# Filling the attention of an even mixer with projection work, on one core of a Trainium2

## The reference, cut to what matters

```python
def even_mixer(h, w_in, gla_w_gate, gla_b_gate, gla_norm_g, fox_b_f, w_out):
    q_g, k_g, v_g, g_out, gk_low, q_f, k_f, v_f, f_logit = jnp.split(h @ w_in, EVEN_SPLITS, axis=-1)
    ...
    o_gla = gla_chunked(q_g, k_g, v_g, gk)                 # 4 heads, values of 128
    o_gla = rmsnorm(o_gla, gla_norm_g) * jax.nn.silu(g_out)  # norm over the 128 values of a head
    log_f = jax.nn.log_sigmoid(f_logit + fox_b_f)
    o_fox = fox_attention(q_f, k_f, v_f, log_f)            # 8 heads of 64, softmax, causal
    o = jnp.concatenate([o_gla, o_fox], axis=-1)
    return o @ w_out

def mixer(u, cos, sin, w_in, w_attn_br, dw_w, dw_b, cln_g, cln_b, w_conv_pw, w_out):
    # second block: attention of 8 heads, a depthwise convolution of 31 taps, two gates
    ...
```

## Time and profile before

| what | value |
|---|---|
| median of three runs | 1800.25 us (1794.48 to 1805.85) |
| time of the profiled execution | 1797.06 us |
| its span | 1795.3 us, 27915 instructions |
| TensorE busy | 1742.4 us (97%) |
| VectorE busy | 1373.1 us (76%) |
| ScalarE busy | 936.6 us (52%) |
| GpSimd busy | 292.9 us (16%) |
| mean DMA rate | 194 GB/s |
| mean granted TensorE clock | 0.986 of full speed |

### The profile page before, as it was taken

The page is one execution under the profiler, slowest core; times in us unless marked ns, Lnnn a source line. Parts: engine busy times, 40 slices in busy tenths (PEclk is TensorE's granted clock), DMA queues, the critical chain, the costliest instruction groups (busy, mean ns, idle before and its releaser), DMA issues.

```text
span 1795.3 us, 27915 instructions
## 1 busy us (share of the span) xinstructions
PE 1742.4 (97%) x11232; PEld 1564.8 (87%) x11232; DVE 1373.1 (76%) x1830; ACT 936.6 (52%) x1172; POOL 292.9 (16%) x219
## 2 busy tenths in 40 slices
PE   6999999999999999999999999999999999999998
PEld 5888798888888888878888898898888998998887
DVE  5997655698888978686987779878755699778654
ACT  6554454655456544466554354656543536555433
POOL 1000000130120001050000139600000089010000
PEclk9999998999999999999999999999999999999999
DMA  7777433277667766523666643343555344335551
GB/s 272 277 253 272 166 143 139 82 289 263 229 257 281 260 241 249 211 94 146 253 258 250 241 165 141 121 165 138 188 194 193 129 148 159 140 121 200 189 193 47
DMA packets 53232, 348.28 MB, mean 194 GB/s; under 512 B 6769, under 2 KB 10114, under 8 KB 13058
## 3 DMA queue, kind: packets, MB, share of 16 engines
q1 hardware_dynamic: 53122, 346.73, 52.9%
HBM read 345.65 MB, written 1.05 MB: 193 GB/s over the span
## 4 chain that ended last, share of the span: by engine, by line
PE 78%; issue 11%; POOL 5%; DVE 3%; ACT 2%; POOLq 0%; DMA 0%; SPq 0%; ACTq 0%; DVEq 0%
PE bank L927 38%; PE bank L926 20%; PE bank L882 5%; PE bank L883 4%; PE bank L884 4%; POOL arena L831 4%; DVE wl L1928 1%; ACT wh L1468 1%; PE bank L897 1%; PE bank L1401 0%; PE bank L1226 0%; PE bank L907 0%; POOL arena L833 0%; DMA raw<-in_chunks 0%; PE bank L1194 0%
## 5 line engine op out<-in xcount | busy, mean ns | idle before, releaser
L1928 DVE TENSOR_TENSOR wl<-raw,wh 128x2048 fp32r<-128x2048 f32 (+1 forms) x279 | 640.0, 2295 | 246.1 <-ACT wh L1468 245.4
L927 PE MATMUL bank<-xx,wh 128*128 128x512 f32 x1920 | 670.5, 393 | 0.0
L1468 ACT ACTIVATE wh<-raw 128x2048 fp32r<-128x2048 f32 (+1 forms) x279 | 526.2, 1886 | 209.8 <-PE bank L927 174.1
L926 PE MATMUL bank<-xx,wl 128*128 128x256 f32 x1920 | 540.7, 282 | 14.8 <-DVE wl L1928 14.8
L927 PEld LDWEIGHTS bank<-xx,wh 128*128 128x128 f32 x1920 | 360.6, 188 | 80.0
L927 PE MATMUL bank<-hx,wh 128*128 128x512 f32 x1216 | 422.0, 390 | 0.0
L926 PEld LDWEIGHTS bank<-xx,wl 128*128 128x128 f32 x1920 | 364.0, 190 | 16.1 <-issue 14.7
L926 PE MATMUL bank<-hx,wl 128*128 128x256 f32 x1216 | 343.4, 282 | 1.2 <-DVE wl L1928 1.2
L882 PE MATMUL bank<-xx,wh 128*128 128x256 f32 x1008 | 293.6, 291 | 2.5 <-ACT arena L1602 1.4
L883 PE MATMUL bank<-xx,wh 128*128 128x256 f32 x1008 | 286.8, 285 | 0.0
L884 PE MATMUL bank<-xx,wl 128*128 128x256 f32 x1008 | 286.7, 284 | 0.0
(11 more groups left out here) (329 smaller groups left out, 1962.6 us busy)
## 6 DMA issues: line engine op xcount, KB each, us to landing
raw<-in_chunks SPq DMA_DIRECT2D x263, 1024.0 KB, 4.8
arena<-in_ada SPq DMA_DIRECT2D x48, 1024.0 KB, 5.0
raw<-in_chunks SPq DMA_DIRECT2D x16, 768.0 KB, 4.2
arena<-in_bias_rows SPq DMA_DIRECT2D x1, 2048.0 KB, 17.6
x<-in_x SPq DMA_DIRECT2D x4, 256.0 KB, 4.1
arena<-in_w_uk SPq DMA_DIRECT2D x1, 1024.0 KB, 4.8
arena<-in_w_uv SPq DMA_DIRECT2D x1, 1024.0 KB, 9.0
out<-x SPq DMA_DIRECT2D x8, 128.0 KB, 2.1
```

The costliest lines, as they stand in the source:

```text
L926: pe.matmul(o[:, 0:T], lo_w, halves[:, 0, :], start=start, stop=False, skip_group_check=True)
L927: return pe.matmul(o.rearrange("p (h t) -> p h t", h=2), hi_w, halves, start=False, stop=stop, skip_group_check=True)
L1468: act.activation(wh[:, c % RING, at], raw[:, c % RING, at], ACT.Copy).then_inc(hi_made.sem, 1)
L1928: dve.tensor_tensor(wl[:, c % RING, at], raw[:, c % RING, at], wh[:, c % RING, at].bitcast(F32), ALU.subtract).then_inc(lo_made.sem, 1)
```

## The change

- **Column norm.** TensorE forms the sums of squares with the squares as weights and one column of ones (eight matmuls of one column), so that they stand as 128 x 8 values. Root and reciprocal are taken of 8 columns. A new step `spread`, after chunk 10, spreads them with eight matmuls (a column broadcast as weights, the identity moving) into banks 4 and 5; ScalarE copies both out, VectorE multiplies as before.
- **Value chunk 11** leaves the list and runs in two halves, after the scores of pair 0 and of pair 1. ScalarE copies it out and runs its `hi` at the end of round 1, VectorE its `lo` in round 2.
- **Output chunks 12 and 13**, tiles k = 0 to 3, run in rounds 2 and 3 and no longer in `pe_out`.
- **Scores** use banks 4 and 5 alone, so that scores of pair p wait for the masks of pair p - 1. `halves` moves behind the loop's first masks on VectorE and ahead of the pairs on ScalarE.
- **Mixers of the second block.** VectorE's `lo` of chunk 19, which stood ahead of the last five taps, runs behind them, next to `lo` of chunk 20.

```diff
-    SCORES = (4, 5, 2, 3)
-    EVEN = ["small", 0, "z", 1, "gk", 2, "G", 3, "decay", 4, 5, "kt", 6, "A", 7, "kv", 8, "o", 9, "norm", 10, 11, "halves"]
+    EVEN = ["small", 0, "z", 1, "gk", 2, "G", 3, "decay", 4, 5, "kt", 6, "A", 7, "kv", 8, "o", 9, "norm", 10, "spread"]
@@ pe_out
-                    if s != "odd" or (ks[0], j) != (0, 0):
+                    if ks[0] > 0 or not (s == "even" or (s == "odd" and j == 0)):
@@ pe_pairs
+            def last_values(m):
+                c = c0 + F_V + 1
+                pe.wait_ge(lo_made.sem, c + 1)
+                pe.wait_ge(proj_out.sem, proj_out.at(s, F_V))
+                ... (24 matmuls of half m into bank 3)
+                if m == 1:
+                    last.then_inc(chunk_used.sem, 1)
             def scores(p):
-                if p >= 2:
-                    pe.wait_ge(ns_made.sem, ns_made.at(s, 2 * p - 2))
+                if p == 0:
+                    pe.wait_ge(proj_out.sem, proj_out.at(s, F_K + 2))
+                    pe.wait_ge(gla_act.sem, G_ACT["orstd"])
+                    pe.wait_ge(fox_split.sem, 2)
+                else:
+                    pe.wait_ge(ns_made.sem, ns_made.at(s, 2 * p))
             def transposes(h):
+                if h == 0:
+                    pe.wait_ge(gla_dve.sem, G_DVE["o"])
             for i in range(pairs + 2):
                 if i < pairs:
                     scores(i)
+                if i < 2:
+                    last_values(i)
+                elif i < 4:
+                    pe.wait_ge(proj_out.sem, proj_out.at(s, F_V + i - 1))
+                    out_part(s, c0 + 12, range(0, 4), i - 2)
@@ pe_even
             def norm():
-                for q in range(2):
-                    last = pe.matmul(bank[4 + q][:, :], ones[:, :], osq[:, q * 512:(q + 1) * 512], start=True, stop=True)
+                for i in range(8):
+                    last = pe.matmul(bank[4][:, i:i + 1], osq[:, i * P:(i + 1) * P], ones[:, 0:1], start=(i == 0), stop=True, ...)
+            def spread_norm():
+                pe.wait_ge(gla_dve.sem, G_DVE["oinv"])
+                for i in range(8):
+                    last = pe.matmul(bank[4 + i // 4][:, (i % 4) * P:(i % 4 + 1) * P], ocol[:, 1, i:i + 1].broadcast_to((P, P)), ident[:, :],
+                                     start=True, stop=True)
-            pe.wait_ge(gla_dve.sem, G_DVE["o"])
-            pe.wait_ge(fox_split.sem, 2)
             pe_pairs(s)
@@ act_pairs
+                if s == "even" and i == 1:
+                    act_chunk(s, F_V + 1, base[s] + F_V + 1)
@@ act_even
-                act.activation(oroot[:, 0:512], bank[4][:, :], ACT.Sqrt, ...)
-                act.activation(oroot[:, 512:1024], bank[5][:, :], ACT.Sqrt, ...)
+                act.activation(ocol[:, 0, :], bank[4][:, 0:8], ACT.Sqrt, ...)
+            def spread_norm():
+                act.wait_ge(gla_pe.sem, G_PE["ospread"])
+                act.activation(orstd[:, 0:512], bank[4][:, :], ACT.Copy)
+                act.activation(orstd[:, 512:1024], bank[5][:, :], ACT.Copy).then_inc(gla_act.sem, 1)
+            halves()
             act_pairs(s)
@@ dve_pairs
+                if s == "even" and i == 0:
+                    halves()
+                if s == "even" and i == 2:
+                    lo(base[s] + F_V + 1 + RING)
@@ dve_even
-                link(dve.reciprocal(orstd, oroot))
+                dve.reciprocal(ocol[:, 1, :], ocol[:, 0, :]).then_inc(gla_dve.sem, 1)
+            def spread_norm():
+                dve.wait_ge(gla_act.sem, G_ACT["orstd"])
                 ... (lines 2216 and 2220 as before)
@@ dve_mix, last round of the attention
-                lo(c0 + 12 + 2 * p + RING)
-                convolve(TAPS_PER_STEP)
                 if p < 2:
+                    lo(c0 + 12 + 2 * p + RING)
+                    convolve(TAPS_PER_STEP)
                     lo(c0 + 13 + 2 * p + RING)
             convolve(len(taps))
             ...
+            lo(c0 + 16 + RING)
             lo(c0 + 17 + RING)
```

More of the change, by code:

```diff
@@ L284, in build @@
     AT = pj[:, 0:2, :]
-    osq, oroot, orstd = Carver(at_z).take(4 * T), Carver(at_e).take(4 * T), Carver(at_k).take(4 * T)
+    osq, ocol, orstd = Carver(at_z).take(4 * T), Carver(at_e).take(16, "p (r i) -> p r i", r=2), Carver(at_k).take(4 * T)
     c = Carver(ARENA - ATT)
@@ L511, in vec @@
         return vecT[:, tile, row:row + 1]
-    G_PE = {n: i + 1 for i, n in enumerate(["z", "G", "kt", "A", "kv", "o", "ostat"])}
-    G_ACT = {n: i + 1 for i, n in enumerate(["glow", "z", "lnz", "lnf", "gs", "decays", "keT", "osq", "oroot"])}
-    G_DVE = {n: i + 1 for i, n in enumerate(["fz", "zabs", "fabs", "gk", "fsum", "decayed", "A", "state", "o"])}
-    EVEN = ["small", 0, "z", 1, "gk", 2, "G", 3, "decay", 4, 5, "kt", 6, "A", 7, "kv", 8, "o", 9, "norm", 10, 11, "halves"]
+    G_PE = {n: i + 1 for i, n in enumerate(["z", "G", "kt", "A", "kv", "o", "ostat", "ospread"])}
+    G_ACT = {n: i + 1 for i, n in enumerate(["glow", "z", "lnz", "lnf", "gs", "decays", "keT", "osq", "oroot", "orstd"])}
+    G_DVE = {n: i + 1 for i, n in enumerate(["fz", "zabs", "fabs", "gk", "fsum", "decayed", "A", "state", "oinv", "o"])}
+    EVEN = ["small", 0, "z", 1, "gk", 2, "G", 3, "decay", 4, 5, "kt", 6, "A", 7, "kv", 8, "o", 9, "norm", 10, "spread"]
     E_K, E_Q, E_V, E_G, F_Q, F_K, F_V = 0, 1, 2, 4, 6, 8, 10
@@ L1057, in pe_pairs @@
             q, k, v, _ = att_of(s)
-            pe.wait_ge(proj_out.sem, proj_out.at(s))
-            def scores(p):
-                if p >= 2:
-                    pe.wait_ge(ns_made.sem, ns_made.at(s, 2 * p - 2))
+            c0 = base[s]
+            def last_values(m):
+                c = c0 + F_V + 1
+                pe.wait_ge(lo_made.sem, c + 1)
+                pe.wait_ge(proj_out.sem, proj_out.at(s, F_V))
+                tok = slice(m * P, (m + 1) * P)
+                for kk in range(KT):
+                    col = slice(kk * T, (kk + 1) * T)
+                    last = three(bank[3][:, m * T:(m + 1) * T], xh[:, kk, tok], xl[:, kk, tok], wh[:, c % RING, col], wl[:, c % RING, col],
+                                 start=(kk == 0), stop=(kk == KT - 1))
+                if m == 1:
+                    last.then_inc(chunk_used.sem, 1)
+            def scores(p):
+                if p == 0:
[4 more added lines that the diff above has]
+                    pe.wait_ge(ns_made.sem, ns_made.at(s, 2 * p))
                 for at, qt, kt in ((slice(0, P), slice(0, P), slice(0, P)), (slice(P, 384), slice(P, T), slice(0, T))):
                     for h in (2 * p, 2 * p + 1):
-                        pe.matmul(bank[SCORES[h % 4]][:, at], q(h)[:, qt], k(h)[:, kt], start=(at.start == 0), stop=False, skip_group_check=True)
+                        pe.matmul(bank[4 + h % 2][:, at], q(h)[:, qt], k(h)[:, kt], start=(at.start == 0), stop=False, skip_group_check=True)
                 for h in (2 * p, 2 * p + 1):
-                    b = bank[SCORES[h % 4]]
+                    b = bank[4 + h % 2]
                     pe.matmul(b[:, 0:384], selr[32:40, h, :], fhigh[32:40, :], start=False, stop=False, skip_group_check=True)
@@ L1080, in output @@
             def output(p):
+                pe.wait_ge(proj_out.sem, proj_out.at(s, F_V + 1 + p // 2))
                 pe.wait_ge(pt_out.sem, pt_out.at(s, 2 * p + 2))
@@ L1167, in norm @@
                 pe.wait_ge(gla_act.sem, G_ACT["osq"])
-                for q in range(2):
-                    last = pe.matmul(bank[4 + q][:, :], ones[:, :], osq[:, q * 512:(q + 1) * 512], start=True, stop=True)
+                for i in range(8):
+                    last = pe.matmul(bank[4][:, i:i + 1], osq[:, i * P:(i + 1) * P], ones[:, 0:1], start=(i == 0), stop=True, skip_group_check=True)
+                last.then_inc(gla_pe.sem, 1)
+            def spread_norm():
[3 more added lines that the diff above has]
+                                     start=True, stop=True)
                 last.then_inc(gla_pe.sem, 1)
             todo = {"small": small, "z": z, "G": cumulate, "kt": turn_keys, "A": scores, "kv": chunk_states,
-                    "o": outputs, "norm": norm}
+                    "o": outputs, "norm": norm, "spread": spread_norm}
             for step in EVEN:
@@ L1706, in halves @@
                                ACT.Copy).then_inc(xh_made.sem, 1)
-            todo = {"small": small, "z": z, "gk": log_sigmoid, "G": cumulated, "decay": decays, "kt": keys, "o": squares, "norm": norm, "halves": halves}
+            todo = {"small": small, "z": z, "gk": log_sigmoid, "G": cumulated, "decay": decays, "kt": keys, "o": squares, "norm": norm, "spread": spread_norm, "halves": halves}
             for step in EVEN:
@@ L2098, in link, with dve_pairs @@
             dve.wait_ge(dve_step.sem, n_step[0])
-        def dve_pairs(s):
+        def dve_pairs(s, halves=None):
             pairs = heads_of[s] // 2
@@ L2110, in masked @@
                 for b, at in enumerate((slice(0, P), slice(P, 384))):
```

(6 more changed lines are left out.)

3 lines of the change are left out of this document (1 added, 2 removed).

## The result

| | before | after |
|---|---|---|
| median of 9 runs | 1798.74 us (1794.48 to 1805.85) | 1787.14 us (1783.61 to 1792.18) |
| profiled execution, its span | 1797.06, 1795.3 us | 1791.12, 1789.4 us |
| mean granted TensorE clock | 0.986 | 0.990 |

The ratio is 0.9932, 95% interval 0.9919 to 0.9944: 10 to 14.6 us faster, where I had forecast 5.8. The two profiled executions differ by 5.9 us only; that half the gain is missing between them is part of what had to be found.

The account below looks back on a forecast made before the run. TensorE, busy 97% of the span, was taken as the bound. Even mixer 3.8 plus second-block mixers 2.0 gave 5.8 us: 1791.3 from the profiled execution, 1794.5 from the median, forecast 1794 us, range 1787 to 1801.

Parts of the forecast that it names:

- the term for the mixers of the second block: Moving `lo` of chunk 19 behind the taps gains 2.0 us in `mix0`, 0 in `mix1`; bounds together 0 and 3.
- The even mixer's 3.8: Even mixer's attention: gain 4.8 us at full clock, less 1.0 for low clock, so 3.8, between 0 and 6.5.
- The loop's end: Even mixer's attention loop ends at 328.1 at full clock; the old position of the same point was 333.1.
- 1.0 for the clock still to come: One low-clock stretch of 3.4 us behind the new wait in the even mixer, at about 7 in 10: -1.0 us.
- first wait: TensorE stands still about 1.9 us before the first scores, until ScalarE has copied the spread out behind `hi`.
- the last outputs' wait: Even mixer: the last outputs wait about 1.0 us for ScalarE to copy out two transposes.
- Column norm, 16 passes: Even mixer, TensorE: new norm's one-column matmuls take 2.0 us against 1.3 before, so +0.7 us; upper bound 2.2.
- The reading of the long stall: Even mixer's 3.25 us idle before the first transposes: VectorE's 6.55 us reciprocal puts `lo` and split late, ahead of the masks.
- Queues, two score banks, softmax beside the rounds: Later loads cost nothing; scores of pair 1 wait 0.3 us for masks; softmax fits beside 6.2 us rounds, 3 us cover.
- Rival A: Nothing to see: same TensorE work, waits return elsewhere; gain -2 to 2.5 us, 1798 to 1802; chance 0.22.
- B: Slower: low clock holds through the even mixer's attention loop; 19 us net, 1819, or 1811 with two thirds; chance 0.06.
- Rival C: More: one-column matmuls nearly free, clock doesn't fall, wait shrinks; gain 8 to 10 us, 1791; chance 0.12.

Follow-up runs that it names:

- e3: Only the move of VectorE's `lo` of chunk 19 behind the last taps in both second-block mixers, on the kernel before: 1793.74 us, ratio 0.9976.
- e2: The change without its last block, so the even mixer changed and the second block's mixers left as before: 1791.47 us, ratio 0.9953 to the kernel before.
- e9: The change plus seven spare 128-column matmuls in the wait before the first scores: 1787.73 us, ratio 0.9943 to the kernel before.
- e1: The kernel before, run again with no edit: 1798.03 us, ratio 0.9994.
- e8: The kernel before plus six spare 128-column matmuls ahead of line 1374 in both second-block mixers: 1794.86 us, ratio 0.9978.
- e5: The kernel before with only the new column norm and its spread: 1799.36 us, ratio 0.9994.
- e6: The change with the old norm, roots and reciprocal over 1024 columns: 1792.57 us, ratio 0.9957 to the kernel before.
- e4: The whole change, run again as it is: 1788.18 us, ratio 0.9940 to the kernel before.
- e10: The kernel before plus spare matmuls in the even mixer's attention, four ahead of the first scores, twelve behind scores(1): 1796.92 us, ratio 1.0003.

## Why the prediction had the mechanism right and the size wrong

The mechanism held and the size did not: 5.8 us forecast, some 11 measured. The step that failed is the term for the mixers of the second block, 2.0 us with `mix1` at 0: they brought 4.2 us in the mean of the traces and 2.5 to 6 in time (e3). The even mixer's 3.8 was too small as well; its stage gained 5.2. By its terms:

1. **Even mixer, 3.8 us forecast, 5.2 in the stage** (6 to 11 in time, e2). The loop's end was placed at 328.1 from a start at 290.3; it came at 328.36 from 290.61. That 328.1 was for full clock, with 1.0 for the clock still to come on top, and it came out right by luck: the low stretch came and cost 1.3 to 1.5 us, more than the 1.0 (e9, and the half chunk at 303.55), but three terms beside it were too dear: norm and first wait by 0.3 and 0.2, the spread by 0.3, the last outputs' wait by 1.0, which was not there since the outputs of pair 2 cover it. So the 1.0 taken off for the clock is most of the 1.4 us by which this term was too small.
2. **Column norm, 16 passes taken at 0.125 us.** They took 1.70 us, 0.106 each (290.61 to 292.31). The exchange cost even less than that saving: chunk 10's copy comes 7.66 us behind the start of the norm before (290.32 to 297.98) and 7.72 after (290.61 to 298.33), so 0.1 us and not 0.7; the old norm had held TensorE longer than the 1.3 that I read. The 1.7 us that the Trainium skill's rule on weight loads had given ("TensorE: Matmul & The Clock Gate", section "LDWEIGHTS (loading the stationary operand)") agree with the trace. The 25 ns floor of the same page ("Wait — 56ns, not 53.3ns?") (0.4 us for the step) does not show where every pass brings new weights. Broadcast weights were no slower than others: 16 spread passes in 1.95 us with the drain.
3. **`mix0`, 2.0 forecast, 2.4 between the first two traces and 2.7 in the mean; `mix1`, 0 forecast, 1.5 in the mean.** This is the term that failed. "ScalarE's squares already start with nothing waited for" was true of the one execution that I read. In e1 the same program waits 1.90 us there, then runs 3.4 us at 0.50, and loses 2.6 us that the change gives back. e3 puts both mixers at 2.5 to 6 us, above my bound of 3 for the most part. e8 shows what I had left out: I had priced the wait and not the low clock behind it.
4. **The reading of the long stall.** "Why the long stall is there" (the reciprocal) named the smaller part: e5 takes the reciprocal away alone and the stage grows by 2.9 us. The first masks start 17.3 us behind the roots' table load before and 18.4 in e5, because `lo` of chunk 14 waits for `hi`, `hi` for chunk 11's copy, and the spread on TensorE puts chunk 11 2 us later. With chunk 11 and `halves` moved and the long reciprocal kept (e6) they start at 14.0, with both (the change) at 12.3.
5. **Queues, two score banks, softmax beside the rounds**: as forecast. No load came late, scores of pair 1 did not wait for the masks (done at 306.7, TensorE there at 308.1; in e9, without the low clock, they waited 0.16 us), and the transposes of pairs 2 and 3 wait for nobody.

Rival A fell, and so did B in its place: the loop ran at 1.00 from 307.3 on. Rival C (8 to 10 us) came nearest in size, and for other reasons: the one-column matmuls were not nearly free, and the clock did fall. The feed-forward rates and the missing loss in `mix1` explain why two single executions showed 5.9 us; the odd mixer (127.3 us in the first trace after, 130.4 in e4, 129.1 before) moves by as much from one execution to the next. The terms give 5.2 + 4.2 = 9.4 us. That lies in the interval of e4 (8 to 13) and just under that of the result (10 to 14.6); what is between was not separated further.

## What to carry to other kernels

A wait of TensorE of 1.7 to 2 us cost its length and, when TensorE ran flat out behind it, in most executions another 1.3 to 2.9 us of low clock; price both, or fill the wait, with real work first and spare matmuls where there is none. Low clock cost next to nothing where TensorE waited for another engine anyway (e10), so look where in the low stretch TensorE is busy. Before a stall is put down to one instruction, ask what that engine would wait for next without it. A reading that sets a term to zero from one execution needs a second execution of the same program.

## What was not expected of the hardware

One program shows two rates of feed-forward matmuls at full clock, 1006 or 993 of them in 174 us, in stretches of 100 us and more, changing from execution to execution. DMA moved 257 and 254 GB/s in the two; in e5 and e10 it moved 259 in both, with 992 and 1006 matmuls, so the rate of DMA doesn't tell them apart. No run here shows the cause. Twelve spare matmuls that compute nothing, six in each mixer, made the kernel faster, by 1.3 to 6.7 us in e8; the kernel before has such matmuls elsewhere (`keep_clock`), and not at this wait.
